# A fifth seven-product chunk pair, and a down projection that adds onto the residual in PSUM

## The reference

```python
f = rmsnorm(h, g_ffn)
h = h + (silu(f @ w_gate) * (f @ w_up)) @ w_down     # w_gate, w_up: 2048 x 5632, w_down: 5632 x 2048
```

## Time and profile before

| what | value |
|---|---|
| median of the runs | 1162.54 us |
| the profiled execution, its own time | 1162.51 us |
| its span, first to last instruction | 1160.7 us |
| TensorE busy | 1147.6 us, 99% |
| VectorE busy | 945.9 us, 81% |
| ScalarE busy | 630.8 us, 54% |
| GpSimd busy | 124.8 us, 11% |
| granted TensorE clock, mean | 0.998 of full speed |

### The profile page before, as it was taken

One profiled execution on the slowest core, in us unless ns is written; L12 is line 12 of the kernel. 1 busy time (PEld: TensorE's weight loads), 2 busy tenths in 40 slices (PEclk: granted clock), 3 DMA queues, 4 the chain that ended last, 5 costly groups with the idle time before them and its releaser, 6 DMA issues.

```text
span 1160.7 us, 16347 instructions
## 1 busy us (share of the span) xinstructions
PE 1147.6 (99%) x5618; PEld 968.9 (83%) x5618; DVE 945.9 (81%) x1272; ACT 630.8 (54%) x809; POOL 124.8 (11%) x74
## 2 busy tenths in 40 slices
PE   9999999999999999999999999999999999999996
PEld 8889989988888877888888888888888888888886
DVE  6689767767777999988989898989989898947674
ACT  6544465466455664746556464647364555647552
POOL 0222443436031000000000000000000000000111
PEclk9999999999999999999999999999999999999999
DMA  9655555454655565664747474745647374754541
GB/s 343 215 182 181 182 182 165 163 179 149 198 170 177 181 237 199 200 234 145 254 143 254 143 253 145 253 162 200 216 153 262 128 272 140 250 201 153 201 160 73
DMA packets 113121, 223.38 MB, mean 192 GB/s; under 512 B 5194, under 2 KB 6418, under 8 KB 112817
## 3 DMA queue, kind: packets, MB, share of 16 engines
q1 hardware_dynamic: 112608, 222.08, 56.4%
q10 hardware_dynamic: 464, 0.66, 0.2%
HBM read 220.63 MB, written 2.10 MB: 192 GB/s over the span
## 4 chain that ended last, share of the span: by engine, by line
PE 92%; DVE 3%; issue 2%; ACT 1%; POOL 1%; POOLq 0%; DVEq 0%; ACTq 0%
PE ps L1423 14%; PE ps L1425 14%; PE ps L1424 14%; PE ps L1626 11%; PE ps L1628 11%; PE ps L1627 11%; PE ps L1457 3%; PE ps L1456 3%; PE ps L1455 3%; PE ps L1465 2%; PE ps L1621 1%; PE ps L1620 1%; PE ps L1619 1%; DVE w_lo L950 1%; PE ps L1432 1%
## 5 line engine op out<-in xcount | busy, mean ns | idle before, releaser
L655 ACT ACTIVATE w_hi<-w_raw 128x1024 fp32r<-128x1024 f32 (+1 forms) x286 | 291.2, 1027 | 272.5 <-PE ps L1425 154.1
L950 DVE TENSOR_TENSOR w_lo<-w_raw,w_hi 128x1024 fp32r<-128x1024 f32 x250 | 301.0, 1216 | 118.5 <-ACT w_hi L655 117.0
L1423 PE MATMUL ps<-w_hi,oT_hi 128*128 128x512 f32 x320 | 125.7, 393 | 0.0
L1425 PE MATMUL ps<-w_hi,oT_lo 128*128 128x512 f32 x320 | 124.6, 390 | 0.0
L1424 PE MATMUL ps<-w_lo,oT_hi 128*128 128x512 f32 x320 | 124.6, 389 | 0.0
L1423 PE MATMUL ps<-w_hi,nT_hi 128*128 128x512 f32 x280 | 111.4, 398 | 0.0
L1425 PE MATMUL ps<-w_hi,nT_lo 128*128 128x512 f32 x280 | 109.2, 390 | 0.0
L1424 PE MATMUL ps<-w_lo,nT_hi 128*128 128x512 f32 x280 | 109.0, 389 | 0.0
L579 POOL TENSOR_TENSOR w_lo<-w_raw,w_hi 128x1024 fp32r<-128x1024 f32 x36 | 86.4, 2399 | 182.3 <-ACT w_hi L655 182.3
L1006 DVE SCALAR_TENSOR_TENSOR ps<-arena,taps,ps 128x256 f32<-128x256 f32 x232 | 94.7, 482 | 0.2 <-ACT ps L776 0.2
L1626 PE MATMUL ps<-w_hi,nT_hi 128*128 128x512 f32 x220 | 86.5, 393 | 0.0
(11 more groups left out here) (278 smaller groups left out, 2579.8 us busy)
## 6 DMA issues: line engine op xcount, KB each, us to landing
w_raw<-in_w_gate SPq DMA_DIRECT2D x88, 512.0 KB, 3.9
w_raw<-in_w_up SPq DMA_DIRECT2D x88, 512.0 KB, 4.8
w_raw<-in_w_down SPq DMA_DIRECT2D x44, 1024.0 KB, 5.1
w_raw<-in_w_in SPq DMA_DIRECT2D x32, 1024.0 KB, 5.1
w_raw<-in_w_out SPq DMA_DIRECT2D x16, 1024.0 KB, 5.0
w_raw<-in_w_pgate SPq DMA_DIRECT2D x16, 1024.0 KB, 5.0
w_raw<-in_w_in SPq DMA_DIRECT2D x14, 512.0 KB, 10.2
w_raw<-in_w_ple SPq DMA_DIRECT2D x2, 1024.0 KB, 6.8
```

The costliest lines, as they stand in the source:

```text
L655: nc.scalar.activation(tiles_of(m)[0], source_of(m), ACT.Copy).then_inc(hi_ready, 1)
L950: nc.vector.tensor_tensor(lo, source_of(m), hi.bitcast(F32), ALU.subtract).then_inc(lo_ready, 1)
L1423: nc.tensor.matmul(banks[t][:, :], x_hi[:, k, rows], hi[:, k], start=start, stop=False)
L1425: ins = nc.tensor.matmul(banks[t][:, :], x_lo[:, k, rows], hi[:, k], start=False, stop=stop)
```

## The change

1. `QUAD_KINDS` becomes PPSSSSSP: pair 4 is done with seven products. A pass has 26 + 8 = 34 units.
2. `LOOP_SLOTS` becomes 7, because the sums of x for the fifth S pair lie where the slot in `oT_hi` and `oT_lo` was. Slots are numbered anew in each pass (34 is no multiple of 7), so the first six units of a pass wait for the unit six before them, the seventh for the one thirteen before, all others for the one seven before.
3. The down projection accumulates onto `h`. ScalarE copies `h` into the two banks of a panel before TensorE starts it (`seed`), TensorE's matmuls all accumulate (`add_tokens_by_columns`), and ScalarE copies the banks back to `h` (`read_back`). `add_down` on VectorE goes. ScalarE's list gets: behind the copies of P1 and P5 the seed of panel 0; one step later the seed of panel 1, which waits for VectorE's second combine; at the steps `DOWN_AT` + 1 and + 3 the reading back of panels 0 and 1 followed by the seeds of 2 and 3; at + 5 the reading back of panel 2, and of panel 3 at the pass's end.

```diff
-QUAD_KINDS = "PPSSPSSP"
+QUAD_KINDS = "PPSSSSSP"
-LOOP_SLOTS = 8
+LOOP_SLOTS = 7
...
-                n = (m - LOOP0) % LOOP_SLOTS
+                n = (m - LOOP0) % PER_LOOP % LOOP_SLOTS
                 if n == 4:
-                    return tuple(o[:, 12:16].rearrange("p (k a) t -> p k (a t)", k=2) for o in (oT_hi, oT_lo))
-                if n == 5:
                     return w_more[:, 0:2], w_more[:, 2:4]
-                if n >= 6:
-                    return w_extra[:, n - 6, 0:2], w_extra[:, n - 6, 2:4]
+                if n > 4:
+                    return w_extra[:, n - 5, 0:2], w_extra[:, n - 5, 2:4]
...
+        def slot_back(m):
+
+            j = (m - LOOP0) % PER_LOOP
+            if j >= LOOP_SLOTS:
+                return LOOP_SLOTS
+            return PER_LOOP - max(k for k in range(PER_LOOP) if k % LOOP_SLOTS == j) + j
+
...
-                engine.wait_ge(half_done, m - LOOP_SLOTS + 1 + PER_LOOP * it)
+                engine.wait_ge(half_done, m - slot_back(m) + 1 + PER_LOOP * it)
             elif PLE0 <= m < PLE0 + SLOTS:
-                engine.wait_ge(half_done, m - LOOP_SLOTS + 1)
+                engine.wait_ge(half_done, m - PER_LOOP % LOOP_SLOTS + 1)
...
+            def seed(c, it, first):
+
+                if c == 0:
+                    sc.wait_ge(product_copied, 2 + 2 * it)
+                elif c == 1:
+                    sc.wait_ge(combined, 2 + 8 * it)
+                else:
+                    sc.wait_ge(h_back, 2 * (c - 1) + 8 * it)
+                if c < 2 and not first:
+                    sc.wait_ge(h_back, 8 * it - 8 + 2 * (c + 1))
+                for t in range(TT):
+                    nc.scalar.activation(DOWN_BANKS[c][t][:, :], h[:, t, c * NP:(c + 1) * NP], ACT.Copy).then_inc(h_seeded, 1)
+
+            def read_back(c, it):
+
+                sc.wait_ge(half_done, LOOP0 + DOWN_AT + 2 * (c + 1) + PER_LOOP * it)
+                for t in range(TT):
+                    nc.scalar.activation(h[:, t, c * NP:(c + 1) * NP], DOWN_BANKS[c][t][:, :], ACT.Copy).then_inc(h_back, 1)
+
...
                         nc.scalar.activation(p5_sum, P5[:, :], ACT.Copy).then_inc(product_copied, 1)
+                        seed(0, it, first)
+                    if t == DOWN_AT - 1:
+                        seed(1, it, first)
+                    if t in (DOWN_AT + 1, DOWN_AT + 3, DOWN_AT + 5):
+                        done = (t - DOWN_AT) // 2
+                        read_back(done, it)
+                        if done < 2:
+                            seed(done + 2, it, first)
...
+                read_back(3, it)
...
-            def add_down(c, it):
-
-                ve.wait_ge(half_done, LOOP0 + DOWN_AT + 2 * (c + 1) + PER_LOOP * it)
-                ve.wait_ge(down_read, 2 * (c + 1) + 8 * it)
-                for t in range(TT):
-                    cols = slice(c * NP, (c + 1) * NP)
-                    nc.vector.tensor_tensor(h[:, t, cols], DOWN_BANKS[c][t][:, :], h[:, t, cols], ALU.add).then_inc(down_read, 1)
-
...
-                    if t in (DOWN_AT + 2, DOWN_AT + 4, DOWN_AT + 6):
-                        add_down((t - DOWN_AT) // 2 - 1, it)
...
-                add_down(3, it)
...
+            def add_tokens_by_columns(m, banks, x_hi, x_lo, last, it):
+
+                arrived(m, it)
+                hi, lo = slot_of(m)
+                for k in range(2):
+                    for t in range(TT):
+                        rows = slice(t * P, (t + 1) * P)
+                        nc.tensor.matmul(banks[t][:, :], x_hi[:, k, rows], hi[:, k], start=False, stop=False, skip_group_check=True)
+                        nc.tensor.matmul(banks[t][:, :], x_hi[:, k, rows], lo[:, k], start=False, stop=False, skip_group_check=True)
+                        ins = nc.tensor.matmul(banks[t][:, :], x_lo[:, k, rows], hi[:, k], start=False, stop=last and k == 1, skip_group_check=True)
+                ins.then_inc(half_done, 1)
...
                 for c in range(4):
-                    if c == 0:
-                        pe.wait_ge(product_copied, 2 + 2 * it)
-                    if c == 1:
-                        pe.wait_ge(combined, 2 + 8 * it)
-                    if c >= 2:
-                        pe.wait_ge(down_read, 8 + 2 * (c - 1) + 8 * it)
+                    pe.wait_ge(h_seeded, 2 * (c + 1) + 8 * it)
```

More of the change, by code:

```diff
@@ L379, in hybrid_decoder_layer @@
         a_hi_ready, a_ready = sem("a_hi_ready"), sem("a_ready")
-        product_copied, combined, down_read = sem("product_copied"), sem("combined"), sem("down_read")
+        product_copied, combined, h_seeded, h_back, rb2_ready = sem("product_copied"), sem("combined"), sem("h_seeded"), sem("h_back"), sem("rb2_ready")
         raw_first = [sem(f"raw_first{i}") for i in range(4)]
@@ L1178, in normalise @@
                 ve.wait_ge(x_joined, i + 1)
-                ve.wait_ge(down_read, 7)
+                ve.wait_ge(rb2_ready, 1)
                 nc.vector.tensor_tensor(x_norm(i), x_norm(i), along_tokens(2), ALU.mult).then_inc(x_normal, 1)
@@ L1241, in _ @@
                     ve.wait_ge(rb_spread, 2)
-                    nc.vector.tensor_copy(rb[:, :], LOW[1][0][:, 0:T]).then_inc(down_read, 7)
+                    nc.vector.tensor_copy(rb[:, :], LOW[1][0][:, 0:T]).then_inc(rb2_ready, 1)
                 for i in range(QUADS):
@@ L1344, in _ @@
                     if m == DOWN0 + 2 * (c + 1):
-                        ve.wait_ge(down_read, 8 * LOOPS + 2 * (c + 1))
+                        ve.wait_ge(h_back, 8 * (LOOPS - 1) + 2 * (c + 1))
                         add_panel(Q_DOWN_LAST + c, c, m)
@@ L1637, in unit_tile, with seven_products @@
                 return hi[:, f], lo[:, f]
-            def seven_products(i, it):
+            def seven_products(i, it, first_pass):
                 at = LOOP0 + QUAD_AT[i]
@@ L1655, in seven_products @@
                 block_product(P5, s1, unit_tile(at + 2, 0), first, last)
-                if first:
-                    pe.wait_ge(down_read, 8 + 8 * it)
+                if first and not first_pass:
+                    pe.wait_ge(h_back, 8 * it)
                 block_product(P7, s3, unit_tile(at + 2, 1), first, last).then_inc(half_done, 1)
@@ L1661, in seven_products, with eight_products @@
                 block_product(P4, x_block(i, 1, 1), unit_tile(at + 3, 1), False, False).then_inc(half_done, 1)
-            def eight_products(i, it):
+            def eight_products(i, it, first_pass):
                 at = LOOP0 + QUAD_AT[i]
                 pe.wait_ge(a_ready, i + 1)
-                if i == 0:
-                    pe.wait_ge(down_read, 6 + 8 * it)
+                if i == 0 and first_pass:
+                    pe.wait_ge(rb2_ready, 1)
+                elif i == 0:
+                    pe.wait_ge(combined, 8 * it - 2)
                 for k in range(2):
@@ L1715, in _, with feed_forward @@
                 gate_and_up(m)
-            def feed_forward(it):
+            def feed_forward(it, first_pass=False):
                 for i in range(QUADS):
                     if QUAD_KINDS[i] == "S":
-                        seven_products(i, it)
+                        seven_products(i, it, first_pass)
                     else:
-                        eight_products(i, it)
+                        eight_products(i, it, first_pass)
                     if i == 0:
+                        if not first_pass:
+                            pe.wait_ge(h_back, 8 * it - 2)
                         turn_act(ACT_BANKS, it)
                 for c in range(4):
-                    if c == 0:
-                        pe.wait_ge(product_copied, 2 + 2 * it)
-                    if c == 1:
-                        pe.wait_ge(combined, 2 + 8 * it)
-                    if c >= 2:
-                        pe.wait_ge(down_read, 8 + 2 * (c - 1) + 8 * it)
+                    pe.wait_ge(h_seeded, 2 * (c + 1) + 8 * it)
                     for k in range(2):
                         rows = slice(2 * k, 2 * k + 2)
-                        tokens_by_columns(LOOP0 + DOWN_AT + 2 * c + k, DOWN_BANKS[c], oT_hi[:, rows], oT_lo[:, rows], k == 0, k == 1, it)
-            feed_forward(0)
+                        add_tokens_by_columns(LOOP0 + DOWN_AT + 2 * c + k, DOWN_BANKS[c], oT_hi[:, rows], oT_lo[:, rows], k == 1, it)
+            feed_forward(0, True)
             with pe.Fori(1, LOOPS - 1) as it:
@@ L1743, in _ @@
                 if c == 0:
-                    pe.wait_ge(down_read, 6 + 8 * LOOPS)
+                    pe.wait_ge(combined, 8 * LOOPS - 2)
+                    pe.wait_ge(h_back, 8 * LOOPS - 2)
                     turn_act(HIGH[0], LOOPS)
                 else:
-                    pe.wait_ge(down_read, 8 + 8 * LOOPS)
+                    pe.wait_ge(h_back, 8 * LOOPS)
                 for k in range(2):
```

4 lines of the change are left out of this document (2 added, 2 removed).

## The result

The changed kernel takes 1182.46 us, the median of four runs (1182.12 to 1183.01), against 1162.53 for the kernel before beside it: a ratio of 1.0173, with a 95% interval of 1.016 to 1.0186. It is 19.9 us slower. The forecast was 1174.5, 12 us slower, in a range of 1169.5 to 1183. Sign and place were right; the loss was forecast too small, and the time lies in the range by half a microsecond only.

A forecast was written before the change was run, and what follows sets the result against it. TensorE, 99% busy, was taken to bound the old kernel, with VectorE falling behind in five S pairs in a row after the change. Sum: 1162.51 + 2.6 + 9.2 = 1174.3, with possible tenths ahead of the loop 1174.5 us; range 1169.5 to 1183.

The forecast's parts named there:

- VectorE loses 1.84 us of its lead on each S pair.: In the S run: VectorE needs 6.60 us for a full S pair, TensorE 4.76.
- Seeds one every 0.50, a record of 0.60: ScalarE's copies of h into PSUM: 0.60 us each, one every 0.50; lower end 0.45, upper end 0.69.
- dear seeds: Rival, 13%: at one seed every 0.69 us, six seeds in the chain add 1.1 a pass; 1186 us.
- Pair 6 late by 1.3, ring 64.2: VectorE delivers unit 22 at 22.2, 1.3 us after TensorE wants it; by unit 22 alone a pass is 64.2 us.
- VectorE runs without a pause: After a 1.19 us hand-over over ScalarE, VectorE works from unit 10 to the first combine without a gap.
- Combines at 32.3, panel 2 at 41.5, pass 64.4: Times after TensorE ends pair 1: first combines start, panel 2 can start; adding 22.9 gives the pass, against 63.45 before.
- the ring: Chain of waits from TensorE's end of pair 1 to the next, over combines, ScalarE's seeds and panel 2: 64.4 us.
- First pass +2.6: VectorE starts without lead, so in the first pass panel 2 starts at 446.5 instead of 443.94.
- If that is too little, it is once, below 1 us.: Ahead of the loop, pair 6's x sums add under 2 us on VectorE; idle time and four units' lead should cover it.
- Everything arrives: Rival, 6%: VectorE's lead lasts and only the saved products count, 6.8 us less: 1155.7 us.
- Only the VectorE cycle: Rival, 18%: copies at 0.45 or less, or shorter hops, leave only unit 22's lateness: pass 64.2, 1172 us.
- A late load: Rival, 6%: panel 2's weights land in 7 us instead of 5.1, shifting ScalarE and the combines by 1: 1184 us.

The follow-up runs named there:

- Number 3: Changed kernel with VectorE's weight sums over 384 of 512 columns, so it doesn't compute the layer: 1165.31 us, ratio 1.0024.
- Number 11: Changed kernel with first two combines one step earlier, x sums of groups 2 and 3 later, weight sums over 256 of 512 columns (layer not computed): 1153.44 us.
- number 4: Changed kernel with VectorE's first two combines one step earlier, ahead of the split of one more down unit: 1177.62 us, ratio 1.0129.
- number 7: Changed kernel with the x sums of groups 2 and 3 made later, ahead of the loop: 1180.60 us, ratio 1.0157.
- experiment 8: Changed kernel with first combines earlier, x sums later, and the lo split of each S pair's third unit on GpSimd: 1246.39 us, ratio 1.072.
- number 9: Changed kernel with four S pairs (PPSSPSSP) instead of five, seven slots and seeding kept: 1219.91 us, ratio 1.0501.

## Why the forecast was right in sign and too small

By the prediction's steps:

- **VectorE loses 1.84 us of its lead on each S pair.** Right: the pairs stand 6.60 and 6.59 us apart. Number 3 shows that the loss hangs on it. Number 11 shows that the change gains when an S pair costs VectorE 5.53.
- **Seeds one every 0.50, a record of 0.60.** Nearly: the median record is 0.594, a pair takes 1.12, so they stand 0.53 apart. The readings have a record of 0.582. They lie between the two bounds, near the chosen value; the "dear seeds" are out. The prediction set the Trainium skill's budget ("ScalarE: Activation LUTs", rules for kernel authors) beside it, an estimated 0.73 us. The Trainium skill gives that budget for an instruction whose bias is a pointer operand, and these copies have none. So the prediction misapplied it, and for them it is too high by 0.14.
- **Pair 6 late by 1.3, ring 64.2.** Place right, ring 64.7 (number 4). The failed step is the sentence "VectorE runs without a pause". ScalarE's split of unit 11 waits 0.30 us for its own slot, and TensorE starts unit 22 at 22.47 (689.19 - 666.72), where 22.2 stood. Another 0.25 us lie behind it, half of them at panel 0, which now waits a little for seed 0 (0.28 us shown at its weight load, about 0.13 by the starts). That is one of the places that the prediction named as proof against it. VectorE's sums hold ScalarE up until 687.51; then it makes seven hi splits back to back (688.47 to 695.11), and seed 0 stands behind them. Three waits at pair 6 came as forecast; they were put at 1.2 us together and are 0.85 in the list, 1.67 by the starts.
- **Combines at 32.3, panel 2 at 41.5, pass 64.4.** The chain was right, link by link, and this is the ring that binds. It measured 32.85 for the combines (mostly VectorE's wait for unit 11 ahead of the S run and its wait of 0.20 for ScalarE at unit 31, 698.42), then 7.94 instead of 7.7 from their end to panel 2, and 22.98 (643.74 to 666.72) instead of 22.9 for the rest. So 65.2 instead of 64.4. The mis-sized term is the time between instructions, 0.8 us a pass: about 0.5 on VectorE's way to the combines, where the sum had none, and 0.25 behind them. I had added up durations from a queue that never ran dry. The four hand-overs behind the combines took 0.3 (0.03 to 0.13 each) where 0.2 stood, and the rest is in the copies.
- **First pass +2.6.** It measured 3.0. That the same waits and hand-overs make up the 0.4 is likely, but wasn't read.
- **"If that is too little, it is once, below 1 us."** Wrong: 1.2 us by the trace, 1.6 to 1.9 by number 7. It was costed by the sum of the operations against VectorE's idle time near the gates (1.22 and 1.05). The idle time lies at 389 us, behind the place; the operations come at 377 to 380, where the next weight unit was already due.
- **The rivals.** "Everything arrives" at 1155.7 is out for this kernel, but number 11 measured what it describes. "Only the VectorE cycle" is out by number 4: taking the other ring away gave 4.8 us. A late load isn't seen: from the first copy of P1 to the tenth the list of waits has none for a load.

So of the 8.0 us that were missing, 6.1 are in the nine passes (15.3 where the sum had 9.2), 1.0 ahead of the loop (1.2 for 0.2), 0.4 in the first pass, and the rest behind the loop and between profile and median. That the time still lies in the range is luck: the upper part of the range stood for dear seeds and a late load, and neither came.

Left open: an order of the pairs that breaks the S run in two (for instance "PSPSSSSP") might give VectorE some lead back in between. It needs another grouping of the x sums and wasn't tried.

## What to carry to other kernels

That TensorE was 98% busy and its feeder VectorE 80% proved nothing here: where the feeder falls behind by 1.84 us an item, the length of the run of such items decides, and its rests elsewhere don't count beyond the lead that the slots hold. When work is moved to an idle engine, look at what is queued behind its new waits: the same two copies cost 1.2 us a pass inside the ring and nothing outside it. A chain through two engines is longer than its durations: here hand-overs took 0.03 to 0.13 us each, a queue that ran dry took 0.2 to 0.3, and each stop of TensorE cost 0.27 more than the wait shown.

## What was not expected of the hardware

- A VectorE operation with both inputs in SBUF that starts during a GpSimd operation of that kind waits for the end of it (0.69 us became 2.74 to 2.77 in 32 sums, experiment 8). The Trainium skill ("SBUF — State Buffer", "SBUF: two separate sides") says of the port pair that both share that whichever starts first gets it for the whole instruction and the other fully blocks; the trace agrees, and shows the other order as well: GpSimd's operation takes 2.40 to 2.41 us in the 18 cases in which no VectorE operation was under way at its start, and 2.65 where VectorE's had started first (701.03 in the rows of experiment 8). VectorE operations that read one input from PSUM were not stretched: those of L1039 in the changed kernel took 0.48 us beside GpSimd's splits ahead of the loop too.
- The mean granted clock was 0.983 in experiment 8 and 0.988 in number 9, against 0.998 in the changed kernel. The changed kernel and the one before have the higher level, 2.4 GHz, throughout, but for the last few microseconds behind TensorE's work. In number 9 the lower one, 1.2 GHz, was granted in five stretches in the loop, 24 us together. Each began during a stop of 3.35 us ahead of panel 3 or at most 1.3 us behind it, and half of these ten stops had none. Inside such a stretch matmuls start 0.43 us apart instead of 0.227. The row is one of them; the first 0.50 is PEclk:

```profile
725.60:732.30 6.70, 5.33 (x13) 4.18 (x14) 1.57 (x3) 1.21 (x3) 0.00 (x0) 0.50 0.50 157
```

  Of the nine distances between copies of P1 in that kernel, three are 69.6, 70.7 and 69.6 us and the other six 68.1 to 68.3. So the clock is at least 5 of its loss of 57 us, and at half the clock for 24 us at most 12. Experiment 8 has eleven such stretches in the loop, 38 us together, the one at 721.8 for instance 0.3 us behind a stop of 2.31; they can be at most 19 of its loss of 84 us.
- A stop of TensorE costs about 0.27 us more than the idle time shown beside it (0.44 for a shown 0.17, 0.67 for a shown 0.41).
